# Two first-kind mixers: input tiles from unnormed x with the norm's factor applied at eviction, and latent norms by token columns

## The reference, cut to what matters

```python
for l in range(2):
    sh1, sc1, g1, sh2, sc2, g2, sh3, sc3, g3 = split(silu(c) @ ada_w[l] + ada_b[l], 9)
    h = rms_norm(x, ffn1_norm[l]) * (1 + sc1) + sh1
    x = x + 0.5 * g1 * swiglu(h, ...)                    # feed-forward part, f = 2l
    h = rms_norm(x, mix_norm[l]) * (1 + sc2) + sh2
    z = h @ w_in[l]                                      # ten tiles of 128 columns
    y_pool = causal_multiscale_pool(z[:, pool part])     # four of the tiles
    y_mla = mla_attention(rms_norm(q latent) @ w_q_b,    # q latent: three tiles
                          rms_norm(kv latent) @ w_kv_b,  # kv latent: two tiles
                          rotary key part)               # one tile
    x = x + g2 * concat(y_pool, y_mla) @ w_out[l]
    h = rms_norm(x, ffn2_norm[l]) * (1 + sc3) + sh3
    x = x + 0.5 * g3 * swiglu(h, ...)                    # feed-forward part, f = 2l + 1
x = rms_norm(x, final_norm)                              # then the hybrid layer, with a fifth swiglu
```

## Time and profile before

| | before |
|---|---|
| median of 3 runs | 1251.41 us (1249.83 to 1252.85) |
| profiled execution | 1254.2 us, its span 1252.3 us |
| TensorE busy | 1235.8 us, 99% |
| VectorE busy | 1014.6 us, 81% |
| ScalarE busy | 611.2 us, 49% |
| GpSimd busy | 133.8 us, 11% |
| granted TensorE clock | 0.996 of full speed |

### The profile page before, as it was taken

How to read it: one execution, slowest core, us unless ns; L and a number is a source line. 1 busy time by engine, 2 the same in 40 slices (tenths; PEclk the granted TensorE clock), 3 DMA queues, 4 the chain that set the end, 5 groups by cost and what they waited for, 6 DMA issues and landing times.

```text
span 1252.3 us, 26836 instructions
## 1 busy us (share of the span) xinstructions
PE 1235.8 (99%) x11387; PEld 1207.3 (96%) x11387; DVE 1014.6 (81%) x1657; ACT 611.2 (49%) x890; POOL 133.8 (11%) x210
## 2 busy tenths in 40 slices
PE   9999999999999999999999999999999999999997
PEld 7999999999999999999999999999999988999997
DVE  4899998788988668999988889899975858766665
ACT  4544344578434647443336685433354476544333
POOL 0111110004111044111110022000001000000000
PEclk9999999999999999999999999999998999999999
DMA  9999998453798653899994435545542432555550
GB/s 368 398 407 383 365 368 320 138 164 103 294 332 332 236 204 130 337 387 345 360 382 163 155 116 184 221 159 195 209 148 85 165 139 85 202 202 202 189 181 35
DMA packets 66103, 293.93 MB, mean 235 GB/s; under 512 B 7744, under 2 KB 8896, under 8 KB 51904
## 3 DMA queue, kind: packets, MB, share of 16 engines
q1 hardware_dynamic: 47552, 225.10, 49.8%
q0 software_dynamic: 18432, 67.12, 13.4%
HBM read 291.14 MB, written 1.05 MB: 233 GB/s over the span
## 4 chain that ended last, share of the span: by engine, by line
PE 87%; DVE 6%; ACT 2%; POOL 1%; DMA 1%; issue 1%; SPq 0%; DVEq 0%; ACTq 0%; POOLq 0%
PE gu_bank L710 16%; PE gu_bank L708 16%; PE gu_bank L709 16%; PE y_bank L708 7%; PE y_bank L710 7%; PE y_bank L709 7%; PE t_bank L708 2%; PE t_bank L710 2%; PE t_bank L709 2%; DVE dn_lo L1971 2%; POOL xn L582 1%; PE gu_bank L760 1%; PE y_bank L734 1%; PE y_bank L1194 1%; DMA ring<-mix_w 1%
## 5 line engine op out<-in xcount | busy, mean ns | idle before, releaser
L708 PE MATMUL gu_bank<-hT_hi,gu_hi 128*128 128x256 f32 x1649 | 456.2, 277 | 0.9 <-DVE hT_lo L1957 0.8
L710 PE MATMUL gu_bank<-hT_hi,gu_lo 128*128 128x256 f32 x1649 | 455.8, 276 | 0.0
L709 PE MATMUL gu_bank<-hT_lo,gu_hi 128*128 128x256 f32 x1649 | 455.8, 276 | 0.0
L708 PEld LDWEIGHTS gu_bank<-hT_hi,gu_hi 128*128 128x128 f32 x1649 | 309.4, 188 | 1.4 <-DVE hT_lo L1957 1.1
L709 PEld LDWEIGHTS gu_bank<-hT_lo,gu_hi 128*128 128x128 f32 x1649 | 309.5, 188 | 0.1
L710 PEld LDWEIGHTS gu_bank<-hT_hi,gu_lo 128*128 128x128 f32 x1649 | 309.5, 188 | 0.0
L1976 DVE TENSOR_TENSOR gu_lo<-raw_gu,gu_hi 128x2048 fp32r<-128x2048 f32 x103 | 236.0, 2292 | 29.5 <-ACT gu_hi L1469 27.4
L1469 ACT ACTIVATE gu_hi<-raw_gu 128x2048 fp32r<-128x2048 f32 x100 | 191.0, 1910 | 35.5 <-DMA raw_gu<-ffn_gu 35.5
L1490 ACT ACTIVATE sg<-gu_bank 128x256 f32<-128x256 f32 x82 | 31.5, 384 | 349.9 <-PE gu_bank L710 349.9
L708 PE MATMUL y_bank<-act_hi,dn_hi 128*128 128x256 f32 x660 | 183.5, 278 | 0.9 <-DVE act_lo L2035 0.9
L709 PE MATMUL y_bank<-act_lo,dn_hi 128*128 128x256 f32 x660 | 182.5, 277 | 0.0
(11 more groups left out here) (561 smaller groups left out, 2240.3 us busy)
## 6 DMA issues: line engine op xcount, KB each, us to landing
raw_gu<-ffn_gu SPq DMA_DIRECT2D x110, 1024.0 KB, 6.9
stage<-ada POOLq DMA_DIRECT2D x128, 512.0 KB, 7.9
raw_dn<-ffn_dn SPq DMA_DIRECT2D x110, 512.0 KB, 4.1
ring<-mix_w SPq DMA_DIRECT2D x72, 512.0 KB, 3.6
stage<-ada SPq DMA_DIRECT2D x8, 512.0 KB, 14.5
pro<-ada SPq DMA_DIRECT2D x6, 512.0 KB, 13.8
x<-x_in SPq DMA_DIRECT2D x1, 1024.0 KB, 5.7
ring<-ada SPq DMA_DIRECT2D x2, 512.0 KB, 17.5
```

The source lines that it names most:

```text
L708: pe.matmul(to, a[0], b[0], start=start, stop=False)
L709: pe.matmul(to, a[0], b[1], start=False, stop=False)
L710: return pe.matmul(to, a[1], b[0], start=False, stop=stop)
```

## The change

- The mixers' norms (kt = 1, 4) take the form that kt = 2, 3, 5 have. `raw_residual`, `raw_halves` and GpSimd's `raw_norm` run for them too; their halves go to `mix_raw_hi` and `mix_raw_lo`, which share memory with `hT`, `hT_hi` and `hT_lo` (the ring is in use there). VectorE's `split(l, 2, 2)` now stands ahead of the residual. `busy`, `sums`, `partial`, `scaled` and `shifted` are gone from this place.
- TensorE starts tiles 0 and 1 chunk by chunk; tile 2 has the token sums behind its third chunk and the rows ahead of its last. All ten tiles have 258 columns in two of three passes.
- Each tile leaves PSUM in two steps: VectorE sums the two extra columns into `z_bias` (128x32, a line of 128 bytes) and writes tile times `rstdT` to SBUF (`z_scale`), then ScalarE squares it with the bias (latent tiles) and adds the bias in place. ScalarE splits unit n + 3 ahead of that.
- The latent norms use token columns: a clearing product and 48 or 32 tiny ones, a root and a reciprocal of 128x2, and a row by `latent_rows` behind tile 5 and tile 8. VectorE's order becomes the one below the diff.
- For kt = 1 to 5 VectorE adds the pairs of squares at the end of `raw_residual` (GpSimd's L584 goes). Ahead of f = 1, 2, 3 both first halves of the down weights are split before the root (ScalarE and VectorE), and the rows stand one chunk earlier.

```diff
+        mix_raw_lo = sb(area, "mix_raw_lo", [P, KC, S], F32R)
+        mix_raw_hi = sb(area, "mix_raw_hi", [P, KC, RAW_ROW], F32R)
...
@@ gpsimd
+            def raw_norm(kt):
                 for c in range(KC):
                     pool.tensor_tensor(sq_x[:, c, :], x[:, c, :], x[:, c, :], ALU.mult).then_inc(sq_done, 1)
-                pool.wait_ge(sq_done, KC * RAW[r] + KC)
-                pool.tensor_tensor(sq_x[:, 0:4, :], sq_x[:, 0:4, :], sq_x[:, 4:8, :], ALU.add).then_inc(part_done, 1)
+                if kt % 3 == 1:
+                    return
...
@@ tensor
+            def raw_product(kt, to, w, c):
+                hi = raw_hi_of(kt)[:, c, 0:S + 2]
+                pe.matmul(to[:, 0:S + 2], w[0], hi, start=c == 0, stop=False)
+                pe.matmul(to[:, 0:S], w[0], raw_lo(kt, c), start=False, stop=False)
+                return pe.matmul(to[:, 0:S + 2], w[1], hi, start=False, stop=c == KC - 1)
...
-                            if h == 0 and c == 4:
-                                rows(RAW[r])
+                            if h == 0 and c == 3:
+                                rows(kt)
...
                 def z_tile(n):
-                    product(tile_bank()[:, 0:S], split_unit(l, n)).then_inc(tile_ps, 1)
+                    to, w = tile_bank(), split_unit(l, n)
+                    for c in range(KC):
+                        if n == 2 and c == 3:
+                            raw_sums(kt)
+                        if n == 2 and c == 7:
+                            rows(kt)
+                        last = raw_product(kt, to, [a[:, tok(c)] for a in w], c)
+                    last.then_inc(tile_ps, 1)
...
+                    clear_rows(yb[a][:, 0:S])
                     for c in chunks:
-                        last = pe.matmul(yb[a][:, 0:S], ones[:, :], sq[:, c, :], start=c == chunks.start, stop=c == chunks.stop - 1)
+                        last = token_columns(yb[a][:, 0:S], c, ones[:, 0:2], c == chunks.stop - 1, sq)
...
-                sums_after_ffn(2 * l)
+                pe.wait_ge(prod_done, FB * (2 * l + 1))
                 pe.wait_ge(masks_loaded, 16)
-                busy(1)
-                rows(3 * l + 1)
-                busy(2)
                 mixer(l)
...
@@ scalar
                 if raw:
                     split_dn(0)
+                    split_dn(1)
                     root(kt)
-                    split_dn(1)
...
                 for n in range(ZT):
-                    split(l, n + SLOTS)
-                    act.wait_ge(tile_ps, base + n + 1)
+                    if n != 1:
+                        split(l, n + SLOTS + (n == 0))
+                    act.wait_ge(z_scaled, ZT * l + n + 1)
+                    to, bias = z_home(n), z_bias[:, n:n + 1]
                     if n < QCH + KVCH:
-                        act.activation(sq[:, n, :], zb[n % 4][:, 0:S], ACT.Square).then_inc(sq_ready, 1)
+                        act.activation(sq[:, n, :], to, ACT.Square, bias=bias).then_inc(sq_ready, 1)
+                    act.activation(to, to, ACT.Identity, bias=bias).then_inc(tile_out, 1)
...
@@ vector
+                dve.wait_ge(sq_done, KC * (k + 1) + KC)
+                dve.tensor_tensor(sq_x[:, 0:4, :], sq_x[:, 0:4, :], sq_x[:, 4:8, :], ALU.add).then_inc(part_done, 1)
...
+                def z_scale(n):
+                    dve.wait_ge(tile_ps, base + n + 1)
+                    dve.reduce_sum(z_bias[:, n:n + 1], zb[n % 4][:, S:S + 2], axis=AX.X)
+                    dve.tensor_tensor(z_home(n), zb[n % 4][:, 0:S], rstdT[:, :], ALU.mult).then_inc(z_scaled, 1)
```

More of the change, by code:

```diff
@@ L396, in ss_bank, with raw_hi_of, raw_lo, raw_banks @@
         def ss_bank(kt):
[L398 to L405, removed]
+            if kt in (0, NORMS):
+                return gu_bank[0][:, 0:S]
+            return (tb[0] if kt % 3 == 0 else yb[0])[:, 0:S]
+        def raw_hi_of(kt):
+            return mix_raw_hi if kt % 3 == 1 else raw_hi
+        def raw_lo(kt, c):
+            if kt % 3 == 1:
+                return mix_raw_lo[:, c, :]
+            return raw_lo_first[:, c, 0:S] if c < KC - 2 else raw_lo_last[:, c - KC + 2, 0:S]
+        def raw_banks(kt, b):
             if b:
                 return gu_bank[1], tb[1]
-            return gu_bank[0], yb[0] if RAW[r] % 3 == 0 else tb[0]
+            return gu_bank[0], yb[0] if kt % 3 == 0 else tb[0]
+        def raw_hi_at(kt):
+            return sum(KC + 1 + (KC if k % 3 != 1 else 0) for k in range(1, kt))
+        def raw_lo_at(kt):
+            return (KC + 1) * (kt - 1)
+        def ht_at(kt):
+            return KC * (kt - (kt + 2) // 3)
         def bank_full(dc, mixer):
@@ L424, in program, with z_home @@
         mix_rstd = ma[:, 1, 0:TT]
+        latent_rows_ps = [yb[a][:, S:2 * S] for a in range(2)]
+        def z_home(n):
+            return upad[:, n - 5, PADT:PADT + S] if 5 <= n < 9 else z[:, min(n, 5), :]
         def yt_out(c):
@@ L437, in program @@
         NORMS = 3 * DEPTH
[L438 to L446, removed]
+        RAW_SCALED = 4 * (NFFN - 2)
+        HT_TOK = ht_at(NORMS) + KC
         Y_TOK = KC * NORMS
@@ L636, in _ @@
         def _(pe):
[L637 to L645, removed]
             def raw_sums(kt):
                 to = ss_bank(kt)
-                pe.wait_ge(part_done, part_at(kt) + 1)
+                pe.wait_ge(part_done, kt)
                 clear_rows(to)
@@ L2134, in root @@
                     dve.wait_ge(lat_rooted, 2 * l + a + 1)
-                    step.then(dve.reciprocal(lat_rms[:, a, :], lat_rms[:, a, :]))
+                    dve.reciprocal(lat_rms[:, a, 0:TT], lat_rms[:, a, 0:TT]).then_inc(lat_done, 1)
                 def latent(a):
                     first, count, at = ((0, QCH, L_QN), (QCH, KVCH, L_KVN))[a]
+                    dve.wait_ge(lat_ss, 4 * l + 2 * a + 2)
                     for c in range(count):
-                        step.did(dve.scalar_tensor_tensor(z[:, first + c, :], z[:, first + c, :], lc[:, at + c:at + c + 1], lat_rms[:, a, :],
+                        step.did(dve.scalar_tensor_tensor(z[:, first + c, :], z[:, first + c, :], lc[:, at + c:at + c + 1], latent_rows_ps[a],
                                                           ALU.mult, ALU.mult))
@@ L2492, in _ @@
                 split(l, 1, 1)
-                residual(3 * l)
                 split(l, 2, 2)
-                normed(3 * l + 1)
+                raw_residual(3 * l + 1)
                 gate(l, 1)
```

217 lines of the change are left out of this document (110 added, 107 removed).

## The result

The kernel after takes **1262.4 us** (median of 6 runs, 1258.5 to 1266.7), the kernel before 1250.9 beside it (6 runs, 1249.8 to 1252.9). The ratio is 1.0092, 95% interval 1.0076 to 1.0108: slower by 11.5 us, where 1250.6 and at most 1253.6 were forecast. The profiled execution has a span of 1261.2 us, 8.9 more than before's 1252.3.

What follows compares the result with a forecast made beforehand. TensorE's norm wait of 4.08 us ahead of each mixer and VectorE's chain deep in it were taken as bounds; +1.2 (mixers) - 1.6 (feed-forward) - 0.4 (spacing) = -0.8 on 1251.4 gave 1250.6 us, range 1247.3 to 1253.6.

Steps and rivals of the forecast that it cites:

- the padded bias buffer: Whole kernel: with the shared memory and the removed `partial` sums, it was put at nothing on a path.
- The third rival: Behind the mixers' unnormed tiles: wide spacing outlasts them, 1252.9 us, or 1263 through whole feed-forward parts; chance 0.08.
- The norm's gap of 4.08 us: TensorE ahead of each mixer: gap gone, tile 0's first product within 0.3 us of the last down product.
- The wait for the third latent square: Mixer, ahead of the latent sums behind tile 3: TensorE newly waits 1.1 us for ScalarE's square.
- Pool sums: Mixer, behind tile 8: start at 247.2 against 246.28 before, some 35 us after the last down product.
- Values: Deep in the mixer: products start at 261.1 against 260.87 before, still released by VectorE's half of unit 14.
- the mixers cost: Both mixers: 0.25 and 0.95 us more than before, together 1.2.
- bank wait of tile 13: Mixer, ahead of the values' wait: 0.6 us, and 0.4 for unit 12's bank, costing nothing.
- The waits for the pair sum and for the second hidden block's half: Feed-forward f = 1, 2, 3: 0.28 us goes three times; 0.42 is given back of each later half's wait.
- the new one at f = 2: Ahead of f = 2: TensorE newly waits 0.4 us for the rows, as VectorE's reciprocal comes later.
- The feed-forward part: Unnormed norms ahead of f = 1, 2, 3: together 1.6 us less, plus up to 0.4 of spacing.
- The first rival: Unnormed products: the 0.119 spacing is not the form's; at 0.114 the time is 1248.4 us; chance 0.12.

Runs made afterwards that it cites:

- bias_256: The whole change with z_bias padded to 256 bytes a partition instead of 128, in the same place: 1249.8 us, ratio 0.9978 to the kernel before.
- mixers_only: The change with z_bias behind all other buffers, less the part on f = 1, 2, 3: 1251.8 us, ratio 0.9993 to the kernel before.
- change_bias_last: The whole change with z_bias allocated behind all other buffers, so every tile keeps its old address: 1249.9 us, ratio 0.9983 to the kernel before.
- pad_64: The kernel before with an unused buffer of 64 bytes a partition where the change puts z_bias: 1293.7 us, ratio 1.0336.
- act_up_256: The change with the gap ahead of act_hi 128 bytes longer (act_hi moved 256, gu_hi 128): median 1265.9 us, ratio 1.008 to the kernel before.
- cols_256: The change with z_bias last, unnormed products cut from 258 to 256 columns, one two-column product a tile: 1252.2 us, ratio 1.0014.
- cols_256_plain: The change with z_bias last, unnormed products cut to 256 columns, no two-column products, shift left out: 1248.8 us, ratio 0.997.

## Why the prediction was wrong, step by step

**The step that failed** is one half sentence: "the padded bias buffer ... cost or give nothing on a path". It was taken as a tile that is written and read off the path. What it does is to move others, and that cost 12.6 us (1262.4 against 1249.8 with 256 bytes, not measured side by side). No term of the sum stood for it, and no row was given for putting it at nothing. The third rival had the right symptom, the wide spacing outlasting its place "through a whole feed-forward part", and even the size (1263), but the wrong cause: f = 0 is wide before any unnormed tile of a mixer has run.

**The other steps held**, as after and bias_256 show, counted from the last down product of each mixer's start:

- The norm's gap of 4.08 us is gone: 0.11 in its place (forecast under 0.3). The wait for the third latent square: 231.67 - 230.49 less a product's 0.12 is 1.06 (forecast 1.1), and it is ScalarE's square that ends it.
- Pool sums 252.72 - 217.65 = 35.07 later (forecast 35.1). Values 48.91 later (forecast 49.0); bias_256 has 48.93 and 48.94, before 48.78 and 48.07. So the mixers cost 0.15 and 0.87 more up to there (forecast 0.25 and 0.95), and mixers_only bears it out with 0.8 to 1.0 (forecast 1.2). In one mixer of each kernel the values wait for VectorE's half, as forecast (the second in after, the first in bias_256), in the other for ScalarE's copy, with nearly the same start: the forecast was right about when and half right about whom.
- In the same way the bank wait of tile 13 is 0.67 long in after and 0.77 in bias_256 (forecast 0.6), that of unit 12 0.24 and 0.33 (forecast 0.4). Both lie ahead of the values' wait and cost nothing.
- The waits for the pair sum and for the second hidden block's half are gone, and the new one at f = 2 is there with 0.46 from start to start (forecast 0.4):

```profile
493.99 0.28 PE L734 MATMUL gu_bank<-raw_hi,gu_lo 128*128 128x258 f32 x1
494.57 0.71 PE L687 MATMUL y_bank<-cst,rstd 128*128 128x128 f32 x4 [0.30 <-DVE rstd L1939]
```

- The feed-forward part: forecast 1.6 and up to 0.4 of spacing, measured 1.9 (1250.7 to 1248.9). One more term was read wrongly, at no cost to the sum: of the 6 ns by which an unnormed product was dearer, 1.9 belong to its two columns and 4.2 to the wide spacing. The first rival was right that most of it is not the form's, and wrong about the gain, since the narrow spacing doesn't come.
- The sum, -0.8 on 1251.4: with the layout mended the change takes 1249.8 to 1249.9. That is 0.9 (change_bias_last) and 2.0 (bias_256) under before beside it, and 0.8 and 1.2 under before's runs with a clock of 0.998 or more. 1250.6 was 0.8 too high, inside the forecast's own range of 1249.2 to 1252.3. Two terms were added up wrongly, by 0.1 each: 240 x 0.006 is 1.4 and not 1.3, and 0.7 less the new wait of 0.4 leaves 0.3 and not 0.2 at f = 2. The 1.3 lay ahead of VectorE's wait and did not enter the sum; with the other, the sum is -0.9.

The Trainium skill ("SBUF — State Buffer", section "SBUF: two separate sides") says that TensorE has ports of its own and never waits for another engine there. Nothing here contradicts that: the distances that count are those between two tiles that TensorE itself reads, and the spacing stays wide while the other engines are idle. But a reader who takes it to mean that places are free is wrong by the 43 us of pad_64.

## What to carry to other kernels

An allocation is an edit of every tile behind it. When a buffer is added ahead of tiles that TensorE streams, keep the distances between weight tiles and streamed tiles modulo 256 bytes (here by padding to 256, or by putting the buffer last), and run once with the buffer alone. When TensorE's busy share stays the same and the time moves, divide a stretch of like products by their count before looking for waits: 113.3 against 117.8 ns was the whole loss. If no more than one part is wanted of this change, it is the feed-forward part with the pair sums on VectorE, which at 1248.9 us is no worse than all of it.

## What was not expected of the hardware

- Products of 128x128 weights by 256 fp32 columns start 113.3 to 113.5, 117.7 to 117.9, or 119.0 to 119.9 ns apart, at a granted clock of 1.00. The slowest level comes where the distance between the two tiles is a multiple of 128 bytes; between the others the layout as a whole decides, in a way that is open.
- The first two levels are states that can last: one layout (act_up_256) has whole parts of 170 us at either, and 1253.6 to 1267.8 us from run to run at mean clocks of 0.998 and 0.999, where bias_256 and change_bias_last spread by 2.
- A single product of two columns ahead of each tile costs some 0.11 us in cols_256's trace: the product behind it starts 0.03 us later, and the one behind that 0.20 in place of 0.12. 32 of them make 3.5 us; the medians, not measured side by side, are 3.4 apart (1252.2 and cols_256_plain's 1248.8), where 64 tiny products and a clearing one take 1.09 together.
